# First attention: memory keys turned in 32x32 blocks on VectorE and moved by 16 transfers of ScalarE's queue

## The chip, the cores and the metric

One of the eight cores of one Trainium2 chip runs the kernel. The metric is the device time of one execution in microseconds (us); lower is better. All times of the trace are counted from the start of its span.

## What is computed

The reference is the trunk of a streaming encoder: 256 tokens of width 1024, two layers, each with a half-step FFN, a mixer with `w_in` and `w_out`, and a second half-step FFN. The mixer of the first layer is a pooling mixer. Beside it, in both layers, four heads of 64 attend to 256 rows of a memory. The change touches this attention in the first layer only:

```python
def memory_attention(q, mem, mem_norm_g, w_mem_kv, q_norm_g, k_norm_g):
    B, M, _ = mem.shape
    kv = rms_norm(mem, mem_norm_g) @ w_mem_kv
    k, v = jnp.split(kv.reshape(B, M, 2 * MEM_HEADS, HEAD_DIM), 2, axis=2)
    q = rms_norm(q, q_norm_g)
    k = rms_norm(k, k_norm_g)
    logits = jnp.einsum('bshd,bmhd->bhsm', q, k).astype(jnp.float32) * (HEAD_DIM ** -0.5)
    p = jax.nn.softmax(logits, axis=-1)
    out = jnp.einsum('bhsm,bmhd->bshd', p.astype(v.dtype), v)
    return out.reshape(B, q.shape[1], MEM_WIDTH)
```

Everything is float32. The score product contracts over the 64 values of a head, so queries and keys must both lie with the head's values on the partitions: that is what turning them is for.

## The kernel before

Each engine runs its own list of instructions, written out by hand in the order of the program, and waits on semaphores for the others. TensorE does the matrix products; every large one is done as three products of a high and a low part of either operand. A weight unit is four 128x512 pieces: SyncE loads it (`w_raw`), ScalarE makes the high part (`high_unit`, line 743), VectorE the low part (`low_unit`, line 1156), in three slots used in rotation.

Tokens are in two tiles of 128 (`t` = 0, 1). The stages around the change are, in TensorE's order:

- `mkv0`: the memory's keys and values. VectorE scales them into `mkv_sb` (`kv_copy`, line 1397), sums the squares of the keys (`head_sums`, lines 1406 and 1407), GpSimd makes the roots (`head_roots`), and VectorE scales the keys in place (`head_scale("mk0")`, line 1415).
- `z0b`: the columns of `w_in` that hold the last part of the pooling input and the memory queries. ScalarE copies them out of PSUM in `z_copy(0, 1, t)`: line 956 is the queries, line 957 the pooling part, and line 957 counts up `z_ready`.
- `z0a`: the other columns, tile 0 then tile 1, each eight chunks `k` of three products (lines 1861 to 1863). Two hooks sit in it. `memory_heads(k)`, in tile 0, turns the queries at `k == 3` with `turn_heads(0)` (four 128x128 transposes, line 2056), for which it waits for `mkv_ready` and for `z_ready` at 2, that is for both `z_copy(0, 1, t)`. At `k == 6` it turns the keys with `turn_heads(1)`. `memory_scores(k)`, in tile 1 at `k == 0`, waits for `headT_ready` at 2 and issues the scores (line 2081).
- Between them `head_copy(y)` on ScalarE (line 926) brings the turned queries (`mqT`) and keys (`mkT`) out of PSUM with their gain, each with one count of `headT_ready`.

The table `HEADTS` lists the blocks that `turn_heads` and `head_copy` handle: the name, the PSUM bank and the gain column; `HEADREADY` lists the blocks for which `head_ready` is counted.

The second layer's shared keys already go the other way: VectorE transposes 32x32 blocks into `ycat` (line 1695), GpSimd moves the blocks with 64 transfers within SBUF (line 721), and `key_copy` on ScalarE brings them into `kT` (line 932).

ScalarE's part of the order of work, which is also the order in which its transfers are issued:

```python
high_unit("z0a", 0)
z_copy(0, 1, 0)
high_unit("z0a", 1)
z_copy(0, 1, 1)
high_unit("out0", 0)
head_copy(0)
head_copy(1)
z_copy(0, 0, 0)
```

Of the kernel before, what the change touches and what calls it, by code (L numbers as in the profile page):

```python
# [11 lines left out]
ACT = mybir.ActivationFunctionType  # L12
# [114 lines left out]

HEADNORMS = ["mk0", "mq0", "k1", "mk1", "qa1", "qm1"]
HEADSUMS = ["mk0", "mq0", "k1", ("qa1", 0), ("qa1", 1), "mk1", ("qm1", 0), ("qm1", 1)]
HEADREADY = ["mk0", "k1", "mk1"]  # L130

HEADTS = [("mq0", 7, 1), ("mk0", 6, 0), ("mk1", 1, 3)]

QUERIES = [(0, 0), (0, 1), (1, 0), (1, 1)]
QUERY_BANK = (6, 7, 1, 3)
# [60 lines left out]
def encoder_kernel(nc, a, out):  # L196

    with ExitStack() as ctx:
        def sb(name, shape, dt=F32):
            return ctx.enter_context(nc.sbuf_tensor(name, shape, dt))  # L200

        def sem(name):
            return ctx.enter_context(nc.semaphore(name))
# [11 lines left out]
        mem_blocks = z[:, :, :].rearrange("p t d -> p (t d)").rearrange("p (k t) -> p k t", t=S)  # L215
        key_blocks = ycat[:, 0, 0:NT * KVH * HD].rearrange("p (t c) -> p t c", t=NT)
        key_rows = ycat[:, 1, :].rearrange("p (n t) -> p n t", n=KVH)
        both = sb("mainT", [P, KC, 2, S], F32R)
        tr_hi = {n: sb(f"{n}T_hi", [P, KC, S], F32R) for n in ("side", "y")}
        tr_lo = {n: sb(f"{n}T_lo", [P, KC, S], F32R) for n in ("side", "y")}  # L220
# [63 lines left out]
        mem_blocks_landed = sem("mem_blocks_landed")  # L284
        mem_blocks_turned = sem("mem_blocks_turned")
        keys_landed = sem("keys_landed")
        consts_landed = sem("consts_landed")
        ident_landed = sem("ident_landed")
        gains_landed = [sem(f"gains_landed{g}") for g in range(2)]
# [443 lines left out]
        def _(act):  # L733
# [32 lines left out]
            def high_unit(name, m, halves=(0, 1)):  # L766
                high(name, UNIT[name, m], unit_part(name, m)[1], halves)
# [150 lines left out]
            def head_copy(y):  # L918

                name, bank, g = HEADTS[y]  # L920
                if y == 0:
                    act.wait_ge(consts_landed, 16 * SMALL_LOADS)
                    act.wait_ge(ones_ready, 5)
                act.wait_ge(head_turned, y + 1)
                src, dst = ps[:, bank, :], mqT if name == "mq0" else mkT
                nc.scalar.activation(dst[:, :, :].rearrange("p n t -> p (n t)"), src, ACT.Copy,
                                     scale=head_gain_col[:, g:g + 1]).then_inc(headT_ready, 1)

            def key_copy():

                act.wait_ge(keys_landed, 16 * KVH * BLOCKS * BLOCKS)
                nc.scalar.activation(kT[:, :, :], key_rows, ACT.Copy, scale=head_gain_col[:, 2:3]).then_inc(headT_ready, 1)
# [13 lines left out]
            def z_copy(l, n, t):  # L946
                norm = "H2" if l == 0 else "H7"
                done = Z_ORDER.index((l, n)) + 1
                product_done(act, t, z_done, done, column_units(f"z{l}{'ab'[n]}", n)[1])
                if done % 2 == 1:  # L950
                    act.wait_ge(row_scaled, row_scaled_no(norm, t))
                scale, src, cols = row_scale(norm, t), ps[:, z_bank(l, t, n), :], slice(n * 512, (n + 1) * 512)
                if l == 0 and n == 0:
                    ins = nc.scalar.activation(zp_hi[:, t, cols], src, ACT.Copy, scale=scale)
                elif l == 0:
                    nc.scalar.activation(z[:, t, MIXER:D], src[:, MIXER - 512:512], ACT.Copy, scale=scale)
                    ins = nc.scalar.activation(zp_hi[:, t, 512:MIXER], src[:, 0:MIXER - 512], ACT.Copy, scale=scale)
                else:
                    ins = nc.scalar.activation(z[:, t, cols], src, ACT.Copy, scale=scale)
                ins.then_inc(z_ready, 1)  # L960
# [95 lines left out]
            high_unit("z0a", 0)  # L1056
            z_copy(0, 1, 0)
            high_unit("z0a", 1)
            z_copy(0, 1, 1)
            high_unit("out0", 0)  # L1060
            head_copy(0)
            head_copy(1)
            z_copy(0, 0, 0)
            table_of(ACT.Exp)
            exponentials(0)
# [49 lines left out]
            z_copy(1, 1, 0)  # L1115
            query_squares(1, 0)
            turned_copy(ACT_COPIED)
            head_copy(2)
            high_unit("out1", 1, (0,))
            query_copy(1, 0)  # L1120
            z_copy(1, 1, 1)
# [19 lines left out]
        def _(dve):  # L1141
# [267 lines left out]
            def head_scale(name):  # L1409

                v = head_view(name)
                nh = v.shape[2]
                rs = head_rs[:, HEADNORMS.index(name), 0:NT * nh].rearrange("p (t n) -> p t n", t=NT)
                dve.wait_ge(head_scaled, head_no(name))
                return nc.vector.tensor_tensor(v, v, rs.unsqueeze(3).to_broadcast([P, NT, nh, HD]), ALU.mult)
# [230 lines left out]
            dve.wait_ge(mkv_ready, NT)  # L1646
            head_sums("mk0")
            low_unit("z0a", 0)
            head_scale("mk0").then_inc(head_ready, 1)
            low_unit("z0a", 1)  # L1650
            dve.wait_ge(z_ready, NT)
            head_sums("mq0")
# [96 lines left out]
        def _(pe):  # L1749
# [537 lines left out]
            def memory_heads(k):  # L2287
                if k == 3:
                    pe.wait_ge(mkv_ready, NT)
                    turn_heads(0)  # L2290
                elif k == 6:
                    turn_heads(1)

            def memory_scores(k):
                if k == 0:
# [43 lines left out]
            def second_turns(k):  # L2339
                if k == 0:  # L2340
                    turn_probs(2)
                elif k == 4:
                    turn_probs(3)
                    turn_heads(2)
                elif k == 6:
                    pe.wait_ge(headT_ready, 4)
                    turn_query(1, 0)
# [81 lines left out]
```

## Time and profile before

| | |
|---|---|
| Median of 3 runs | 908.78 us (908.64 to 908.98) |
| Profiled execution: time | 909.13 us |
| Profiled execution: span | 906.9 us |
| TensorE busy | 901.7 us, 99% of the span |
| VectorE busy | 643.2 us, 71% |
| ScalarE busy | 500.8 us, 55% |
| GpSimd busy | 108.8 us, 12% |
| TensorE's share of the chain that ended last | 99% |

The time of an execution is 2.2 us more than its span; the span runs from the first to the last instruction of the trace. A busy share of 99% says that TensorE has matrix products under way nearly always, not that each is at its peak. The chain that ended last is followed back from the last instruction, at each step to what released it.

### The profile page before, as it was taken

To read this page: it belongs to the slowest core of one execution; us is meant where nothing else is said; L and a number is where in the kernel's file an instruction comes from. 1 tells how busy PE (TensorE), PEld (TensorE's weight loads), DVE (VectorE), ACT (ScalarE), POOL (GpSimd) and SP (SyncE) were. 2 spreads that over 40 slices of the span, in tenths; PEclk is the share of its full clock that TensorE was granted. 3 is DMA by queue.
4 is the path that set the end of the run, shared out by engine and by line. 5 is a ranking of instruction groups with operands and counts; after the bars stand their busy time and mean duration, and the time that the engine had idled before them with its cause. 6 is when DMAs were issued, how large, how long until landed. Compare 5 with 4: busy or idle time off the path is not lost.

```text
span 906.9 us, 15027 instructions
## 1 busy us (share of the span) xinstructions
PE 901.7 (99%) x4965; PEld 766.9 (85%) x4965; DVE 643.2 (71%) x1006; ACT 500.8 (55%) x749; POOL 108.8 (12%) x187
## 2 busy tenths in 40 slices
PE   9999999999999999999999999999999999999998
PEld 6888888888888888888888888888888888888887
DVE  6876567687678766566788766666888786666665
ACT  7654545565655554454564645445686664544542
POOL 2153302003000000000002930000132000000000
PEclk9999999999999999999999999999999999999999
DMA  9897666656346656565465865655443276565551
GB/s 303 260 294 219 197 194 177 193 161 203 91 140 206 213 174 196 185 193 194 123 210 165 265 203 166 218 187 182 143 140 118 86 244 215 175 210 189 172 169 47
DMA packets 140180, 168.27 MB, mean 186 GB/s; under 512 B 12472, under 2 KB 104608, under 8 KB 140144
## 3 DMA queue, kind: packets, MB, share of 16 engines
q1 hardware_dynamic: 135600, 164.67, 57.0%
q0 software_dynamic: 4368, 3.07, 1.6%
q8 instruction: 20, 0.33, 0.1%
q14 instruction: 16, 0.13, 0.0%
q10 hardware_dynamic: 176, 0.07, 0.0%
HBM read 166.19 MB, written 1.05 MB: 184 GB/s over the span
## 4 chain that ended last, share of the span: by engine, by line
PE 99%; DVE 1%; ACT 0%; issue 0%; POOL 0%; POOLq 0%
PE ps L1779 35%; PE ps L1784 18%; PE ps L1988 8%; PE ps L1986 8%; PE ps L1984 8%; PE ps L1861 5%; PE ps L1863 5%; PE ps L1862 5%; PE ps L1754 1%; PE ps L2112 1%; PE ps L2216 1%; PE ps L1818 1%; PE ps L2270 0%; PE ps L2081 0%; PE ps L1832 0%; PE ps L2124 0%
## 5 line engine op out<-in xcount | busy, mean ns | idle before, releaser
L1779 PE MATMUL ps<-mainT,w_hi 128*128 128x512 f32 x1376 | 467.7, 392 | 0.1
L1156 DVE TENSOR_TENSOR w_lo<-w_raw,w_hi 128x1024 fp32r<-128x1024 f32 x296 | 350.5, 1221 | 41.3 <-ACT w_hi L743 40.9
L1784 PE MATMUL ps<-mainT,w_lo 128*128 128x256 f32 x1376 | 350.5, 280 | 0.0
L743 ACT CAST w_hi<-w_raw 128x1024 fp32r<-128x1024 f32 x296 | 299.4, 1047 | 29.2 <-PE ps L1779 11.0
L1779 PEld LDWEIGHTS ps<-mainT,w_hi 128*128 128x128 f32 x1376 | 249.2, 187 | 46.1 <-issue 0.5
L1784 PEld LDWEIGHTS ps<-mainT,w_lo 128*128 128x128 f32 x1376 | 255.9, 189 | 13.8
L814 ACT COPY gate_up_f<-ps 128x512 f32<-128x512 f32 x88 | 51.1, 581 | 109.7 <-PE ps L1779 104.0
L1988 PE MATMUL ps<-w_hi,actT_lo 128*128 128x512 f32 x320 | 98.9, 390 | 0.0
L1986 PE MATMUL ps<-w_lo,actT_hi 128*128 128x512 f32 x320 | 98.9, 390 | 0.0
L1984 PE MATMUL ps<-w_hi,actT_hi 128*128 128x512 f32 x320 | 98.6, 389 | 0.0
L1258 DVE TENSOR_TENSOR gate_up_f<-ps,gate_up_f 128x256 f32<-128x256 f32 x88 | 37.3, 423 | 86.1 <-ACT gate_up_f L814 86.0
L820 ACT ACTIVATE gate_up_f<-gate_up_f 128x256 f32<-128x256 f32 x88 | 36.7, 418 | 106.2 <-DVE gate_up_f L1267 106.1
L1281 DVE TENSOR_TENSOR actT_lo<-gate_up_f,actT_hi 128x512 fp32r<-128x512 f32 x40 | 27.7, 692 | 63.9 <-ACT actT_hi L827 63.9
L1988 PEld LDWEIGHTS ps<-w_hi,actT_lo 128*128 128x128 f32 x320 | 60.1, 188 | 12.9
L1986 PEld LDWEIGHTS ps<-w_lo,actT_hi 128*128 128x128 f32 x320 | 60.1, 188 | 12.6
L1984 PEld LDWEIGHTS ps<-w_hi,actT_hi 128*128 128x128 f32 x320 | 60.1, 188 | 11.5
L827 ACT CAST actT_hi<-gate_up_f 128x512 fp32r<-128x512 f32 x40 | 24.8, 620 | 75.1 <-PE ps L1988 69.8
L635 POOL TENSOR_SCALAR row_ms<-row_ss 128x1 f32<-128x1 f32 x14 | 4.9, 349 | 439.8 <-ACT probs L784 439.7
L1275 DVE SCALAR_TENSOR_TENSOR gate_up_f<-gate_up_f 128x256 f32<-128x256 f32 x88 | 37.1, 422 | 22.9 <-ACT gate_up_f L820 22.7
L1267 DVE TENSOR_TENSOR gate_up_f<-gate_up_f,pT 128x256 f32<-128x256 f32 x88 | 36.5, 416 | 0.0
L1260 DVE TENSOR_TENSOR gate_up_f<-ps,gate_up_f 128x256 f32<-128x256 f32 x88 | 36.5, 415 | 0.0
L721 POOL DMA_DIRECT2D ycat<-ycat x64 | 33.9, 538 | 3.0 <-DVE ycat L1695 3.0
(250 smaller groups left out, 845.6 us busy)
## 6 DMA issues: line engine op xcount, KB each, us to landing
w_raw<-in_ffn_w_gate_up_dram SPq DMA_DIRECT2D x352, 256.0 KB, 3.9
w_raw<-in_ffn_w_down_dram SPq DMA_DIRECT2D x176, 256.0 KB, 3.4
w_raw<-in_w_in_dram SPq DMA_DIRECT2D x32, 256.0 KB, 3.4
w_raw<-in_w_out_dram SPq DMA_DIRECT2D x32, 256.0 KB, 3.3
w_raw<-in_w_mem_kv_dram SPq DMA_DIRECT2D x16, 256.0 KB, 3.2
w_raw<-in_w_kv_dram SPq DMA_DIRECT2D x8, 256.0 KB, 3.6
ycat<-in_mem_dram SPq DMA_DIRECT2D x1, 1024.0 KB, 9.0
z<-in_mem_dram POOLq DMA_DIRECT2D x32, 32.0 KB, 4.0
```

The source lines that it names most:

```text
L743: ins = nc.scalar.copy(half(w_hi[s], b), half(w_raw[s], b))
L814: nc.scalar.copy(gate_up_f[:, :, fb, :], ps[:, GU_BANK + 2 * fb:GU_BANK + 2 * fb + 2, S:2 * S]).then_inc(parts_copied, 1)
L1156: ins = nc.vector.tensor_tensor(half(w_lo[s], b), half(w_raw[s], b), half(w_hi[s], b).bitcast(F32), ALU.subtract)
L1258: nc.vector.tensor_tensor(silu_g[:, fb, :], ps[:, bank, 0:S], silu_g[:, fb, :], ALU.add).then_inc(gate_summed, 1)
L1779: return pe.matmul(gate_sums(fb, j)[:, :, tokens], w_hi[units[k // 4][0]][:, k % 4, cols], both[:, k, :, tokens], start=start, stop=stop)
L1784: return pe.matmul(gate_sums(fb, j)[:, 0, tokens], w_lo[units[k // 4][0]][:, k % 4, cols], both[:, k, 0, tokens], start=False, stop=False)
L1861: pe.matmul(dst, x_hi, wh, start=start, stop=False)
L1862: pe.matmul(dst, x_hi, wl, start=False, stop=False)
L1863: return pe.matmul(dst, x_lo, wh, start=False, stop=stop)
L1984: pe.matmul(dst[n], xh, wh[n], start=first and fc == 0, stop=False)
L1986: pe.matmul(dst[n], xh, wl[n], start=False, stop=False)
L1988: mm = pe.matmul(dst[n], xl, wh[n], start=False, stop=closes and (t, n) == (1, 1))
```

## The change

After `head_scale` VectorE transposes the keys of the first attention in 32x32 blocks, all 128x512 of them in one instruction, into the first half of `ycat`. ScalarE then issues 16 transfers of one block row and column each (32 partitions, 4 runs of 32 values, 128 bytes a run) that put the blocks in their place in the second half of `ycat`, and copies them with the gain into `mkT`. The four transposes of the keys on TensorE and the `head_copy` of them go. The transfers are issued between `high_unit("z0a", 1)` and `z_copy(0, 1, 1)`. Where `HEADTS` and `HEADREADY` lose an entry, the numbers of the later entries move up by one; the counts of `headT_ready` stay as they were.

```diff
@@ -127,9 +127,9 @@
 
 HEADNORMS = ["mk0", "mq0", "k1", "mk1", "qa1", "qm1"]
 HEADSUMS = ["mk0", "mq0", "k1", ("qa1", 0), ("qa1", 1), "mk1", ("qm1", 0), ("qm1", 1)]
-HEADREADY = ["mk0", "k1", "mk1"]
-
-HEADTS = [("mq0", 7, 1), ("mk0", 6, 0), ("mk1", 1, 3)]
+HEADREADY = ["k1", "mk1"]
+
+HEADTS = [("mq0", 7, 1), ("mk1", 1, 3)]
 
 QUERIES = [(0, 0), (0, 1), (1, 0), (1, 1)]
 QUERY_BANK = (6, 7, 1, 3)
@@ -215,6 +215,8 @@
         mem_blocks = z[:, :, :].rearrange("p t d -> p (t d)").rearrange("p (k t) -> p k t", t=S)
         key_blocks = ycat[:, 0, 0:NT * KVH * HD].rearrange("p (t c) -> p t c", t=NT)
         key_rows = ycat[:, 1, :].rearrange("p (n t) -> p n t", n=KVH)
+        memory_blocks = ycat[:, 0, 0:NT * MEMH * HD].rearrange("p (n c) -> p n c", c=P)
+        memory_rows = ycat[:, 1, 0:NT * MEMH * HD].rearrange("p (n c) -> p n c", c=P)
         both = sb("mainT", [P, KC, 2, S], F32R)
         tr_hi = {n: sb(f"{n}T_hi", [P, KC, S], F32R) for n in ("side", "y")}
         tr_lo = {n: sb(f"{n}T_lo", [P, KC, S], F32R) for n in ("side", "y")}
@@ -284,6 +286,8 @@
         mem_blocks_landed = sem("mem_blocks_landed")
         mem_blocks_turned = sem("mem_blocks_turned")
         keys_landed = sem("keys_landed")
+        memory_keys_turned = sem("memory_keys_turned")
+        memory_keys_landed = sem("memory_keys_landed")
         consts_landed = sem("consts_landed")
         ident_landed = sem("ident_landed")
         gains_landed = [sem(f"gains_landed{g}") for g in range(2)]
@@ -926,6 +930,22 @@
                 nc.scalar.activation(dst[:, :, :].rearrange("p n t -> p (n t)"), src, ACT.Copy,
                                      scale=head_gain_col[:, g:g + 1]).then_inc(headT_ready, 1)
 
+            def memory_keys():
+
+                act.wait_ge(memory_keys_turned, 1)
+                for i in range(BLOCKS):
+                    for j in range(BLOCKS):
+                        nc.scalar.dma_start(memory_rows[j * BLOCK:(j + 1) * BLOCK, :, i * BLOCK:(i + 1) * BLOCK],
+                                            memory_blocks[i * BLOCK:(i + 1) * BLOCK, :, j * BLOCK:(j + 1) * BLOCK]).then_inc(
+                            memory_keys_landed, 16)
+
+            def memory_key_copy():
+
+                act.wait_ge(memory_keys_landed, 16 * BLOCKS * BLOCKS)
+                nc.scalar.activation(mkT[:, :, :].rearrange("p n (t c) -> p t n c", t=NT),
+                                     memory_rows.rearrange("p (t n) c -> p t n c", t=NT), ACT.Copy,
+                                     scale=head_gain_col[:, 0:1]).then_inc(headT_ready, 1)
+
             def key_copy():
 
                 act.wait_ge(keys_landed, 16 * KVH * BLOCKS * BLOCKS)
@@ -1056,10 +1076,11 @@
             high_unit("z0a", 0)
             z_copy(0, 1, 0)
             high_unit("z0a", 1)
+            memory_keys()
             z_copy(0, 1, 1)
             high_unit("out0", 0)
             head_copy(0)
-            head_copy(1)
+            memory_key_copy()
             z_copy(0, 0, 0)
             table_of(ACT.Exp)
             exponentials(0)
@@ -1115,7 +1136,7 @@
             z_copy(1, 1, 0)
             query_squares(1, 0)
             turned_copy(ACT_COPIED)
-            head_copy(2)
+            head_copy(1)
             high_unit("out1", 1, (0,))
             query_copy(1, 0)
             z_copy(1, 1, 1)
@@ -1646,7 +1667,9 @@
             dve.wait_ge(mkv_ready, NT)
             head_sums("mk0")
             low_unit("z0a", 0)
-            head_scale("mk0").then_inc(head_ready, 1)
+            link(head_scale("mk0"))
+            nc.vector.transpose(memory_blocks.rearrange("p (t n) c -> p t (n c)", t=NT),
+                                mkv_sb[:, :, 0:MEMH * HD]).then_inc(memory_keys_turned, 1)
             low_unit("z0a", 1)
             dve.wait_ge(z_ready, NT)
             head_sums("mq0")
@@ -2288,8 +2311,6 @@
                 if k == 3:
                     pe.wait_ge(mkv_ready, NT)
                     turn_heads(0)
-                elif k == 6:
-                    turn_heads(1)
 
             def memory_scores(k):
                 if k == 0:
@@ -2341,7 +2362,7 @@
                     turn_probs(2)
                 elif k == 4:
                     turn_probs(3)
-                    turn_heads(2)
+                    turn_heads(1)
                 elif k == 6:
                     pe.wait_ge(headT_ready, 4)
                     turn_query(1, 0)
```

ScalarE's list at the place of the change, before. Line 956 with line 957 is `z_copy(0, 1, 1)`, line 743 `high_unit`, line 926 `head_copy`:

```order
L743 CAST w_hi<-w_raw 128x1024 [waits weights_used0,raw_landed00]
L743 CAST w_hi<-w_raw 128x1024 [waits weights_used0,raw_landed01]
L956 ACTIVATE z<-ps,row_rs 128x256 [waits row_scaled,weights_used1]
L957 ACTIVATE yT_hi<-ps,row_rs 128x256
L743 CAST w_hi<-w_raw 128x1024 [waits weights_used1,raw_landed10]
L743 CAST w_hi<-w_raw 128x1024 [waits weights_used1,raw_landed11]
L926 ACTIVATE mqT<-ps,head_gain_col 128x512 [waits head_turned,ones_ready,consts_landed]
L926 ACTIVATE mkT<-ps,head_gain_col 128x512 [waits head_turned]
L954 ACTIVATE yT_hi<-ps,row_rs 128x512 [waits z_done]
```

The same place in the change. Its lines 976 and 977 are `z_copy(0, 1, 1)`, line 747 `high_unit`, line 938 `memory_keys`, line 930 `head_copy(0)`, line 945 `memory_key_copy`:

```order
L747 CAST w_hi<-w_raw 128x1024 [waits weights_used0,raw_landed00]
L747 CAST w_hi<-w_raw 128x1024 [waits weights_used0,raw_landed01]
L938 DMA ycat<-ycat 32x4x32 [waits memory_keys_turned]
L938 DMA ycat<-ycat 32x4x32 x15
L976 ACTIVATE z<-ps,row_rs 128x256 [waits row_scaled,weights_used1]
L977 ACTIVATE yT_hi<-ps,row_rs 128x256
L747 CAST w_hi<-w_raw 128x1024 [waits weights_used1,raw_landed10]
L747 CAST w_hi<-w_raw 128x1024 [waits weights_used1,raw_landed11]
L930 ACTIVATE mqT<-ps,head_gain_col 128x512 [waits head_turned,ones_ready,consts_landed]
L945 ACTIVATE mkT<-ycat,head_gain_col 128x2x2x128 [waits memory_keys_landed]
L974 ACTIVATE yT_hi<-ps,row_rs 128x512 [waits z_done]
```

The sixteen transfers stand ahead of `z_copy(0, 1, 1)`, which counts up `z_ready`; the copy of the keys waits for their landing and no longer for TensorE.

TensorE's list in `z0a`, tile 0, around the hooks of chunk 3 and chunk 6, before. Line 2056 is `turn_heads`, here of the keys; lines 1861 to 1863 are the products:

```order
L1863 MATMUL ps<-w_hi,mainT 128x512
L2056 MATMUL ps<-ident,mkv_sb 128x128 [waits head_ready]
L2056 MATMUL ps<-ident,mkv_sb 128x128 x3
L1861 MATMUL ps<-w_hi,mainT 128x512 [waits lo_ready0]
L1862 MATMUL ps<-w_lo,mainT 128x512
L1863 MATMUL ps<-w_hi,mainT 128x512
```

The same stretch in the change, where line 2079 is `turn_heads` and lines 1884 to 1886 are the products, and behind it the hook of chunk 3, three chunks earlier:

```order
L1884 MATMUL ps<-w_hi,mainT 128x512
L1885 MATMUL ps<-w_lo,mainT 128x512
L1886 MATMUL ps<-w_hi,mainT 128x512
L1884 MATMUL ps<-w_hi,mainT 128x512 [waits lo_ready0]
L1885 MATMUL ps<-w_lo,mainT 128x512
L1886 MATMUL ps<-w_hi,mainT 128x512
```

```order
L1886 MATMUL ps<-w_hi,mainT 128x512
L2079 MATMUL ps<-ident,z 128x128 [waits z_ready,mkv_ready]
L2079 MATMUL ps<-ident,z 128x128 x3
L1884 MATMUL ps<-w_hi,mainT 128x512
L1885 MATMUL ps<-w_lo,mainT 128x512
L1886 MATMUL ps<-w_hi,mainT 128x512
```

The four transposes of the keys and their wait for `head_ready` are gone. The four transposes of the queries, with their wait for `z_ready`, stand where they stood before.

VectorE's list in the change, where line 1436 is `head_scale("mk0")`, line 1671 the new transpose of 32x32 blocks and line 1177 `low_unit`:

```order
L1177 TENSOR_TENSOR w_lo<-w_raw,w_hi 128x1024 [waits hi_ready2] x2
L1436 TENSOR_TENSOR mkv_sb<-mkv_sb,head_rs 128x2x256 [waits head_scaled]
L1671 STREAM_TRANSPOSE ycat<-mkv_sb 128x512 [waits dve_step]
L1177 TENSOR_TENSOR w_lo<-w_raw,w_hi 128x1024 [waits hi_ready0] x2
L1427 TENSOR_TENSOR gate_up_f<-z 128x512 [waits z_ready]
```

Before, `low_unit("z0a", 1)` followed on `head_scale` directly; one instruction, with a wait for VectorE's own `head_scale`, is added between them.

## Rows read from the trace of the kernel before

**Rows 1.** Chain of waits that ended last, share of the span by engine.

```profile
PE 99%; DVE 1%; ACT 0%; issue 0%; POOL 0%; POOLq 0%
```

**Rows 2.** Timeline, ScalarE: start us, us, engine line op, tiles, count [idle before <-releaser].

```profile
212.91 1.05 ACT L743 CAST w_hi<-w_raw 128x1024 fp32r<-128x1024 f32 x1 [0.31 <-PE ps L1863]
215.58 0.47 ACT L956 ACTIVATE z<-ps,row_rs 128x256 f32<-128x256 f32 x1 [1.61 <-PE ps L1863]
215.95 0.47 ACT L957 ACTIVATE yT_hi<-ps,row_rs 128x256 fp32r<-128x256 f32 x1
216.31 1.99 ACT L743 CAST w_hi<-w_raw 128x1024 fp32r<-128x1024 f32 x2
218.19 0.70 ACT L926 ACTIVATE mqT<-ps,head_gain_col 128x512 f32<-128x512 f32 x1
220.58 0.69 ACT L926 ACTIVATE mkT<-ps,head_gain_col 128x512 f32<-128x512 f32 x1 [1.69 <-PE ps L2056]
```

**Rows 3.** Timeline, TensorE, z0a tile 0 to the scores, and the start of out0.

```profile
217.19 0.39 PE L1863 MATMUL ps<-w_hi,mainT 128*128 128x512 f32 x1
217.42 0.60 PE L2056 MATMUL ps<-ident,z 128*128 128x128 f32 x4
...
219.94 0.60 PE L2056 MATMUL ps<-ident,mkv_sb 128*128 128x128 f32 x4
220.30 0.48 PE L1861 MATMUL ps<-w_hi,mainT 128*128 128x512 f32 x1
220.62 0.39 PE L1862 MATMUL ps<-w_lo,mainT 128*128 128x512 f32 x1
220.85 0.40 PE L1863 MATMUL ps<-w_hi,mainT 128*128 128x512 f32 x1
...
221.87 2.00 PE L2081 MATMUL ps<-mkT,mqT 64*128 64x256 f32 x16
...
241.06 0.50 PE L1861 MATMUL ps<-w_hi,yT_hi 128*128 128x512 f32 x1
```

**Rows 4.** Timeline, VectorE, keys to the first maximum of the scores.

```profile
210.80 1.08 DVE L1415 TENSOR_TENSOR mkv_sb<-mkv_sb,head_rs 128x512 f32<-128x512 f32 x1 [1.54 <-POOL head_rs L647]
212.63 2.59 DVE L1156 TENSOR_TENSOR w_lo<-w_raw,w_hi 128x1024 fp32r<-128x1024 f32 x2 [0.76 <-ACT w_hi L743]
216.45 0.69 DVE L1406 TENSOR_TENSOR gate_up_f<-z 128x512 f32<-128x512 f32 x1 [1.23 <-ACT yT_hi L957]
...
223.08 1.23 DVE L1496 TENSOR_REDUCE row_max<-ps 128x4 f32<-128x1024 f32 x1 [2.17 <-PE ps L2081]
```

**Rows 5.** One line's instructions, line 1695: count, ns min/median/max, when.

```profile
L1695 DVE STREAM_TRANSPOSE ycat<-kv_sb x1: 711/711/711, 494.9 to 494.9; 128x512 f32<-128x512 f32 x1
```

**Rows 6.** The same view, lines 1004 and 1005: transfers issued on ScalarE's queue.

```profile
L1004 ACTq DMA_DIRECT2D ident<-in_c_ident_dram x1: 403/403/403, 0.7 to 0.7; - x1
DMA to landing us min/median/max: 2.7/2.7/2.7
L1005 ACTq DMA_DIRECT2D pT<-in_ffn_norm_dram x1: 447/447/447, 1.2 to 1.2; - x1
```

**Rows 7.** Timeline, SyncE and ScalarE: back-to-back issues, and what follows them.

```profile
1.65 1.28 ACT L1007 ACT_TABLE_LOAD   x1 [1.65 <-PEq L2419]
8.95 4.79 SPq L540 DMA_DIRECT2D w_raw<-in_ffn_w_gate_up_dram  x8
```

**Rows 8.** One line's instructions, line 540: transfers on SyncE's queue.

```profile
L540 SPq DMA_DIRECT2D w_raw<-in_w_out_dram x32: 327/380/440, 203.8 to 684.0; - x32
```

**Rows 9.** One line's instructions, line 721: the 64 transfers within SBUF.

```profile
L721 POOL DMA_DIRECT2D ycat<-ycat x64: 536/536/647, 495.9 to 529.2; - x64
DMA to landing us min/median/max: 1.6/3.1/4.4
```

**Rows 10.** Transfers by line and size: tiles, queue, count, KB each, us to landing.

```profile
ident<-in_c_ident_dram ACTq DMA_DIRECT2D x1, 64.0 KB, 2.7
pT<-in_ffn_norm_dram ACTq DMA_DIRECT2D x1, 8.0 KB, 2.6
```

**Rows 11.** Chain of waits that ended last, start of the kernel: start us, us, what.

```profile
1.32 2.74 PE ps L2270 x6
5.32 1.34 PE ps L2270 x4
```

**Rows 12.** Windows: stretch, us, busy (x) of PE, PEld, DVE, ACT, POOL, PEclk, DMA, GB/s.

```profile
2.00:3.00 1.00, 1.00 (x4) 0.30 (x2) 0.00 (x0) 0.99 (x2) 0.73 (x2) 1.00 0.70 231
217.40:221.90 4.50, 4.50 (x26) 3.49 (x24) 3.51 (x5) 2.18 (x3) 1.84 (x2) 1.00 0.47 154
```

**Rows 13.** Waits from 8 to 16 us: who for whom, us, times, longest.

```profile
PE ps L1818 <- DVE mainT L1194: 0.8, 1, 0.8
```

## The prediction

> **What bounds the kernel now.** I read the page first: TensorE carries 99% of the chain that ended last [rows 1]. So whatever takes TensorE's time, or makes it stand still, is paid in full, and work of the other engines costs only where TensorE ends up waiting for it. Next I read the timelines of the three engines between 210 and 224 us. TensorE [rows 3] runs through without a gap: products, the four transposes of the queries at 217.42, more products, the four transposes of the keys at 219.94, and the scores at 221.87. ScalarE [rows 2] is what it has to be watched against. It is often idle there, but its idle time lies in places: it is free at 213.96 (212.91 + 1.05) and next works at 215.58, on `z_copy(0, 1, 1)`, whose second part ends at 216.42 (215.95 + 0.47). TensorE asks for that result at 217.42. The margin between them is 1.0 us, and this number decides the case. VectorE [rows 4] scales the keys until 211.88 and is then idle until 212.63.
>
> **What the change removes.** The four transposes of the keys go from TensorE's own list. They and the slower start behind them take from 219.94 to the third product at 220.85 minus two products of 0.227 us (the pitch of the rows without transposes, for instance 217.19 to 217.42): 0.91 - 0.46 = 0.45 us. All of it is on the path: **-0.45 us**. The `head_copy` of the keys on ScalarE (0.69 us) goes too, and a copy of the same size from SBUF takes its place; I take 0.7 us for it. No gain or loss there, since ScalarE waited 1.69 us ahead of it [rows 2].
>
> **What it adds on VectorE.** One transpose of 128x512 in 32x32 blocks. The same instruction on the other keys took 0.711 us [rows 5]. It runs from 211.9, when `head_scale` has ended, to about 212.65. The next instruction started at 212.63, after 0.76 us of idle time, so it slips by less than 0.1 us, and its result, which ended at 215.22, is wanted by TensorE only for chunk 4, behind the transposes of 217.42 [rows 3, 4]. Cost nothing. If that cover were gone, the price would be the 0.75 us.
>
> **What it adds on ScalarE.** The blocks are turned at about 212.65, before ScalarE arrives at 213.96, so it finds its semaphore up and begins to issue at once. Sixteen issues stand between 213.96 and `z_copy(0, 1, 1)`. What does one cost? The two transfers that ScalarE issued itself took 0.403 and 0.447 us, the second began at 1.2 us and the next instruction of the engine started at 1.65, right behind it [rows 6, 7]: ScalarE is held for the whole of an issue and does nothing else meanwhile. On SyncE single issues took 0.327 to 0.440 us, and eight back to back 4.79 us, 0.60 each, at a time when large loads filled the DMA engines [rows 7, 8]. GpSimd's 64 transfers of the same kind took 0.536 each [rows 9], but GpSimd is another engine. These are the bounds: 0.33 and 0.60 us. I take 0.44 with the gap to the next, as the rows of the same queue are nearest. Sixteen of them are 7.0 us, so `z_copy(0, 1, 1)` starts at 221.0 instead of 215.58. It takes 0.84 us (215.58 to 216.42), and TensorE sees `z_ready` at about 221.9.
>
> The Trainium skill (DMA: Bandwidth & Descriptors, Issuing engines are not separate DMA queues) says otherwise: the sequencer's time to start a DMA "is usually small relative to the DMA itself". Taken as a reason to count the issues at nothing, it would make the whole sum -0.45 us, and 908.3 us in all.
>
> **The stall.** TensorE stands at the hook of chunk 3 from 217.42 to 221.9: **+4.5 us**. Everything behind it on TensorE waits too: the rest of `z0a`, the scores, the pooling. From there the chain of the first attention is 217.42 to 221.87 less the removed 0.45, so 4.0 us, and the scores can start at 225.9.
>
> **Is something else late then?** Four things move with ScalarE, and each is compared with 225.9 or what follows it.
> - The copies. `high_unit("out0", 0)` 221.85 to 223.7 and the copy of the queries to 224.4 come first [rows 2]. The last transfer is issued at 220.6. ScalarE's own transfer landed 2.7 us after its issue [rows 6], those within SBUF after 1.6 to 4.4 us, median 3.1 [rows 9]: 223.3 to 225.0. The copy of the keys then ends at 225.1 to 225.7. Hidden, with 0.2 to 0.8 us to spare.
> - VectorE. Its `head_sums("mq0")` waited for the same `z_copy` and moves by 5.4 us; the first maximum had 2.17 us of idle time before it [rows 4], and moves by 4.05 with TensorE. 2.17 - (5.4 - 4.05) leaves 0.8 us. Hidden.
> - GpSimd's roots of the queries are needed at the end of that maximum, later still. Hidden.
> - SyncE's loads of `out0` move with the low parts on VectorE by 5.4 us; those units are used from 241 us on [rows 3]. Hidden.
>
> **Sum.** 4.5 - 0.45 = +4.05 us. Against the profiled execution, 909.13 + 4.05 = 913.2; that execution is 0.35 us above the median of the runs, so the median after is 908.78 + 4.05 = **912.8 us**, 0.45% slower. With the bounds of one issue: 16 x 0.33 gives +2.3 us (911.1), 16 x 0.60 gives +6.6 (915.4). About 0.2%, or 1.8 us, is what a measurement of this kernel can tell from no change.
>
> **Rivals.**
>
> *An issue is cheap for ScalarE (not slower).* If the queue took transfers without holding the engine, `z_copy` would not be late. The point is 0.156 us an issue: (216.5 - 213.96)/16. Below it the change gains its 0.45 us, 908.3. Up to 0.30 us an issue the loss is within 1.8 us. For it: the transfers are small, 16 KB each, where the loads are 256 KB. Against it: ScalarE's transfers of 64 and 8 KB took 0.403 and 0.447 us, so size hardly matters [rows 6, 10]. Chance 8%. The rule of the Trainium skill's page DMA: Bandwidth & Descriptors that is quoted above would lead to this case; two rows of this very queue speak against it.
>
> *The clock of TensorE falls in the stall.* No row shows a standstill of such length: the longest behind the first microseconds is 0.8 us [rows 13], and the granted clock is 1.00, the 2.4 GHz level, throughout [rows 12]. But at the very start, when TensorE comes from rest, six products of 128x512 took 2.74 us, 0.46 each, against 0.227 later, and the four that followed 1.34 us [rows 11], though the granted clock reads 1.00 there too [rows 12]. Products at half pace cost 2.74 - 6 x 0.227 = 1.4 us and 1.34 - 0.91 = 0.4 us, about 2 us with the transposes between. If the stall does the same, the time is 912.8 + 2 = 914.8 us. The Trainium skill (TensorE: Matmul & The Clock Gate, Why this matters for your kernels) warns of idle gaps between bursts for this reason, and by it this case is the one to expect once the gap is long enough; no row here says whether 4.5 us are. Chance 27%.
>
> *The landing is late.* Sixteen transfers of 128 runs of 128 bytes share the DMA engines with SyncE's loads. If the last lands over 4.5 us after its issue, the scores wait for `mkT`; each microsecond later costs one. With 6 us it would be +5.5, 914.3. The 64 transfers of the other keys landed within 4.4 us beside SyncE's loads [rows 9]. Chance 8%.
>
> *A partial fall of the cost*, between 0.16 and 0.30 us an issue, is in the first rival's 8%. The forecast itself, with issues of 0.33 to 0.60 us and nothing else late, has 57%.
>
> **Numbers.** Range 911.1 to 916.0: the low end is the cheapest issue that a row shows, the high end the clock's fall behind issues of about 0.5 us. Below it lies most of the first rival, above it a fall of the clock with the dearest issues. Slower by over 0.2%: 57 + 27 + 8 = 92%, less 1 for ends of these cases near the bound: 91%. Within 0.2%: 8%. Faster: 1%, since the whole gain in sight is 0.45 us.
>
> **What would show it.** In the profile after: 16 issues on ScalarE's queue from about 214 to 221 us; `z_copy(0, 1, 1)` at 221.0; TensorE idle for about 4.5 us ahead of the transposes of `z`, released by ScalarE's copy; scores right behind `z0a`'s tile 0 with no gap of their own; VectorE's `head_sums("mq0")` idle for over 5 us before. The forecast is wrong in its main step if the issues take under 0.3 us each, or if `z_copy` starts before they are done. The granted clock behind the stall, and the pitch of the products (0.227 or about 0.46 us), decide on the clock. A wait of line 2104 for the copy of the keys would decide for the late landing.

## The result, and the profile after

The changed kernel takes 918.11 us (median of 4 runs, 917.21 to 918.45) against 908.88 us before (4 runs, 908.64 to 909.46). The ratio is 1.0098 with a 95% interval of 1.0086 to 1.011: 9.2 us slower. The prediction was 912.8 us with a range to 916.0. It had the sign and the place, and less than half of the size.

| | before | after |
|---|---|---|
| Profiled execution: time | 909.13 us | 918.41 us |
| Profiled execution: span | 906.9 us | 916.2 us |
| TensorE's share of the chain that ended last | 99% | 97%, and 1% ScalarE's queue |
| Issues on ScalarE's queue in the first attention | none | 16, together 10.95 us |
| Mean granted clock of TensorE | 1.000 | 0.994 |

Timeline of ScalarE after (columns as in [rows 2], to which these rows answer; `ACTq` is its queue of transfers):

```profile
212.66 1.06 ACT L747 CAST w_hi<-w_raw 128x1024 fp32r<-128x1024 f32 x1 [0.30 <-PE ps L1886]
212.68 10.95 ACTq L938 DMA_DIRECT2D ycat<-ycat  x16
223.74 0.47 ACT L976 ACTIVATE z<-ps,row_rs 128x256 f32<-128x256 f32 x1 [10.02 <-issue]
...
226.93 0.73 ACT L945 ACTIVATE mkT<-ycat,head_gain_col 128x512 f32<-128x512 f32 x1
```

The instructions of line 938 (count, ns min/median/max, when):

```profile
L938 ACTq DMA_DIRECT2D ycat<-ycat x16: 608/623/754, 212.7 to 223.0; - x16
...
DMA to landing us min/median/max: 1.8/2.2/3.7
```

One issue took 0.62 us, and from one to the next it is 10.95/16 = 0.684 us. From the end of the cast (212.66 + 1.06 = 213.72) on ScalarE computed nothing until the issues were through: `z_copy(0, 1, 1)` began at 223.74, where it had begun at 215.58 [rows 2]. The issues began at 212.68, while the cast that stands ahead of them in the list was still running. So the first issue does not wait for the arithmetic ahead of it, but what stands behind the issues waits for all of them.

Timeline of TensorE after (it answers to [rows 3]):

```profile
216.94 0.39 PE L1886 MATMUL ps<-w_hi,mainT 128*128 128x512 f32 x1
224.72 1.08 PE L2079 MATMUL ps<-ident,z 128*128 128x128 f32 x4 [7.40 <-ACT yT_hi L977]
...
226.03 0.63 PE L1885 MATMUL ps<-w_lo,mainT 128*128 128x512 f32 x1
226.46 0.63 PE L1886 MATMUL ps<-w_hi,mainT 128*128 128x512 f32 x1
...
230.44 0.39 PE L1884 MATMUL ps<-w_hi,mainT 128*128 128x512 f32 x1
230.67 0.40 PE L1885 MATMUL ps<-w_lo,mainT 128*128 128x512 f32 x1
...
231.23 2.00 PE L2104 MATMUL ps<-mkT,mqT 64*128 64x256 f32 x16
```

And its windows of one microsecond (columns as in [rows 12]; the granted clock stands behind POOL's count):

```profile
219.00:220.00 1.00, 0.00 (x0) 0.00 (x0) 0.00 (x0) 0.00 (x0) 0.00 (x0) 0.92 0.38 84
220.00:221.00 1.00, 0.00 (x0) 0.00 (x0) 0.00 (x0) 0.00 (x0) 0.00 (x0) 0.50 0.20 30
...
229.00:230.00 1.00, 1.00 (x4) 0.79 (x3) 0.08 (x1) 0.00 (x0) 0.00 (x0) 0.50 0.85 295
230.00:231.00 1.00, 1.00 (x6) 0.73 (x4) 0.00 (x0) 0.00 (x0) 0.00 (x0) 0.96 0.77 277
```

TensorE was due for the transposes of the queries at 217.17 (216.94 + 0.227), stood still until 224.72, and then worked at a pitch of 0.43 us a product until about 230, and at 0.23 again from there. The granted clock went from 1.00 (2.4 GHz) to 0.50 (1.2 GHz) just before 220, with TensorE idle, and came back at about 230, after some 5 us of products.

This gives the account of the stretch from the transposes to the scores. Before it lasted 221.87 - 217.42 = 4.45 us [rows 3]. After, counted from when it was due, 231.23 - 217.17 = 14.06 us. The difference of 9.61 us is a standstill of 224.72 - 217.17 = 7.55, less 0.45 for the transposes that went, and what is left is 2.51 us of slow transposes and products. The profiled execution came to this stretch 0.25 us earlier than the one before, and 9.61 - 0.25 = 9.4 agrees with the difference of the spans, 9.3. Nothing worth naming is gained or lost behind the scores.

### The profile page after: what moved, and what is told of

It reads as the page before. It is cut to its first block, busy times and chain, and to the rows that moved or that the text cites. A ratio compares the mean times of both kernels' runs of the same rounds, so it can differ in the third digit from the quotient of the medians.

```text
span 916.2 us, 15036 instructions
## 1 busy us (share of the span) xinstructions
PE 903.5 (99%) x4961; PEld 768.1 (84%) x4961; DVE 643.7 (70%) x1007; ACT 501.1 (55%) x749; POOL 108.8 (12%) x187
## 4 chain that ended last, share of the span: by engine, by line
PE 97%; ACTq 1%; DVE 1%; ACT 0%; issue 0%; POOL 0%; POOLq 0%
PE ps L1802 34%; PE ps L1807 18%; PE ps L2011 8%; PE ps L2009 8%; PE ps L2007 8%; PE ps L1884 5%; PE ps L1886 5%; PE ps L1885 5%; PE ps L1777 1%; ACTq L938 1%; PE ps L2135 1%; PE ps L1841 1%; PE ps L2239 1%; PE ps L2104 0%; PE ps L1855 0%; PE ps L2293 0%
```

## The experiments

All are edits of the changed kernel, so line numbers of theirs are near its own. The ratios are to the kernel before. The theory under test, A, is the account above: ScalarE is held for 0.68 us by each issue, TensorE stands still for a result behind them, and the clock falls in the standstill.

### TensorE kept at work in the standstill

```diff
                 if k == 3:
                     pe.wait_ge(mkv_ready, NT)
+                    keep_warm(32)
                     turn_heads(0)
```

> The change with 32 dummy products (128x512, zeros, into a free PSUM bank) on TensorE right ahead of the turning of the queries, where it stands still. They take 32 x 0.227 = 7.3 us and fit in the standstill of 7.4 us. Theory A (the products behind the standstill ran at half pace only because the clock fell while TensorE was idle): the granted clock stays 1.00, the products behind keep the 0.227 us pitch, and the time falls by 2.5 us against the change, to 915.6 us. Theory B (the slow pace comes from what the other engines do when they all start again): the clock or the pitch is as slow as before behind the dummies, and the time stays at 918.1 us.

Measured: 915.91 us (ratio 1.0075, 1.0059 to 1.0092), 2.2 us less than the change. TensorE's timeline and one of its windows:

```profile
217.48 6.85 PE L2293 MATMUL ps<-probs 128*128 128x512 bf16 x31
224.57 0.66 PE L2079 MATMUL ps<-ident,z 128*128 128x128 f32 x4 [0.24 <-ACT yT_hi L977]
...
228.60 2.00 PE L2104 MATMUL ps<-mkT,mqT 64*128 64x256 f32 x16
```

```profile
224.00:226.00 2.00, 1.75 (x10) 1.25 (x9) 1.41 (x3) 2.00 (x4) 0.00 (x0) 1.00 0.05 8
```

The first line is the dummy products. The transposes begin at nearly the same time as in the change, since ScalarE is as late, but the clock stays at 1.00 and the scores follow 4.03 us behind (228.60 - 224.57) and not 6.51. So 2.5 us of the loss in the profiled execution are the clock's (2.2 us between the medians), and theory B, that the other engines slow TensorE down, is out.

### Fewer transfers

```diff
                 for i in range(BLOCKS):
-                    for j in range(BLOCKS):
+                    for j in (i ^ 1, i ^ 2):
...
-                act.wait_ge(memory_keys_landed, 16 * BLOCKS * BLOCKS)
+                act.wait_ge(memory_keys_landed, 16 * 8)
```

> The change with 8 of the 16 transfers (the blocks on the diagonal and those three off it are left out, so half of the keys do not reach their place). Theory A (every issue holds ScalarE for 0.68 us and that alone makes the standstill): z_copy starts 5.5 us after the first issue instead of 11.1, TensorE stands still for about 2.1 us instead of 7.4, the clock stays at 1.00 in so short a standstill, and the time is 908.9 + 2.1 - 0.45 = 910.5 us. Theory C (a fixed cost of the first transfers, or of the wait for the turned blocks, makes most of it): the standstill falls by clearly less than 5.5 us and the time stays above 912.

With twelve, `j` runs over `(i ^ 1, i ^ 2, i ^ 3)`:

> The change with 12 of the 16 transfers (the blocks on the diagonal are left out, a quarter of the keys). Theory A: a standstill of 7.5 - 4 x 0.68 = 4.8 us, about the one the prediction had. If the clock falls in it, as it fell about 2.6 us after the last product in the change, the time is 908.9 + 4.8 - 0.45 + 2.5 = 915.7 us or a little less; if a standstill of that length leaves the clock alone, 913.2 us. Theory C: above 916.

Measured: eight transfers 910.53 us (ratio 1.0016, 1.0006 to 1.0025), twelve 915.98 us (1.0073, 1.0056 to 1.009). Timelines of ScalarE and TensorE with eight, then with twelve:

```profile
213.21 5.30 ACTq L938 DMA_DIRECT2D ycat<-ycat  x8
...
217.47 0.39 PE L1886 MATMUL ps<-w_hi,mainT 128*128 128x512 f32 x1
219.60 0.63 PE L2079 MATMUL ps<-ident,z 128*128 128x128 f32 x4 [1.75 <-ACT yT_hi L977]
...
223.60 2.00 PE L2104 MATMUL ps<-mkT,mqT 64*128 64x256 f32 x16
```

```profile
213.76 8.21 ACTq L938 DMA_DIRECT2D ycat<-ycat  x12
...
218.01 0.39 PE L1886 MATMUL ps<-w_hi,mainT 128*128 128x512 f32 x1
223.06 1.09 PE L2079 MATMUL ps<-ident,z 128*128 128x128 f32 x4 [4.66 <-ACT yT_hi L977]
...
228.99 2.00 PE L2104 MATMUL ps<-mkT,mqT 64*128 64x256 f32 x16
```

Eight issues take 5.30 us and twelve 8.21: 0.66 and 0.68 each, so the cost is per issue, with no fixed part that shows, and theory C is out. The standstills, by the starts, are 1.9 us and 4.8 us. The clock, a window in the short one and then two in the long one:

```profile
219.00:220.00 1.00, 0.40 (x5) 0.43 (x5) 0.51 (x1) 1.00 (x3) 0.00 (x0) 1.00 0.85 239
```

```profile
220.00:221.00 1.00, 0.00 (x0) 0.00 (x0) 0.00 (x0) 0.00 (x0) 0.00 (x0) 0.68 0.71 165
221.00:222.00 1.00, 0.00 (x0) 0.00 (x0) 0.00 (x0) 0.00 (x0) 0.00 (x0) 0.50 0.21 33
```

Over the short standstill it stayed at 1.00, and the time is what theory A gave, 910.5. In the long one, which has about the length that the prediction had reckoned with, it fell. From the transposes to the scores it took 223.60 - 219.60 = 4.00 us with eight and 228.99 - 223.06 = 5.93 with twelve, so the fall cost 1.9 us here. The 915.7 expected for twelve reckoned with 2.5; that 915.98 came out near it is in part luck, for the profiled execution had also come to the stretch 0.8 us later than the one before.

### What one issue costs

```diff
-                for i in range(BLOCKS):
-                    for j in range(BLOCKS):
-                        nc.scalar.dma_start(memory_rows[j * BLOCK:(j + 1) * BLOCK, :, i * BLOCK:(i + 1) * BLOCK],
...
+                for k in range(3):
+                    nc.scalar.dma_start(memory_rows[k * BLOCK:(k + 1) * BLOCK, :, 0:BLOCK],
+                                        memory_blocks[0:BLOCK, :, k * BLOCK:(k + 1) * BLOCK]).then_inc(memory_keys_landed, 16)
...
+                for k in range(3):
+                    nc.scalar.dma_start(ycat[32:64, 1, 512 + k * P:512 + (k + 1) * P],
+                                        a["mem"][0][0:BLOCK, k * P:(k + 1) * P]).then_inc(memory_keys_landed, 16)
```

> The change with 21 transfers in seven forms, three each, in place of the 16 (the keys do not reach their place; what is measured is what an issue of each form takes on ScalarE's queue). Theory D (the price comes from several runs a partition on both sides): about 0.62 us with 4 runs of 128 bytes a partition on both sides, less with one side in one run, about 0.4 with one run on either side, whether 32 or 128 partitions, SBUF or DRAM. Theory E (it comes from SBUF as the source): 0.62 for all that stay within SBUF, 0.4 for the two that read DRAM. Theory F (it comes from the number of descriptors, 128 a transfer): 0.62 for the forms with 128 runs, and clearly less for 32 runs of 512 bytes; against it stands the transfer of the identity, 128 runs at 0.403 us.

The instructions by line, in the order of issue. Lines 937 to 949 stay within SBUF: the change's own form; 4 runs a partition into one; 32 partitions with one run of 512 bytes; 128 partitions with 128 bytes; 128 partitions with 512 bytes. Lines 952 and 955 read DRAM, with one run and with 4 runs a partition:

```profile
L937 ACTq DMA_DIRECT2D ycat<-ycat x3: 616/635/772, 213.1 to 214.6; - x3
L940 ACTq DMA_DIRECT2D ycat<-ycat x3: 622/623/624, 215.2 to 216.5; - x3
L943 ACTq DMA_DIRECT2D ycat<-ycat x3: 612/612/620, 217.2 to 218.5; - x3
L946 ACTq DMA_DIRECT2D ycat<-ycat x3: 472/616/627, 219.1 to 220.7; - x3
L949 ACTq DMA_DIRECT2D ycat<-ycat x3: 622/622/623, 221.2 to 222.5; - x3
L952 ACTq DMA_DIRECT2D ycat<-in_mem_dram x3: 437/443/603, 223.2 to 224.3; - x3
L955 ACTq DMA_DIRECT2D ycat<-in_mem_dram x3: 445/453/453, 224.8 to 225.7; - x3
```

Neither the runs nor the partitions nor the bytes matter by the medians; theories D and F are out. What is left is whether DRAM is on one side, or else the time of the issue, since those from DRAM stood last. A single execution took 920.83 us, with 21 issues ahead of `z_copy`.

The same with the order turned round, and a store to DRAM added:

> Transfers in five forms, three each, on ScalarE's queue in place of the 16, now with those that read DRAM first, while SyncE loads weights, and the change's own form last (the keys do not reach their place). The first such run gave 0.62 us for every form from SBUF to SBUF and 0.44 for the two from DRAM, but those stood last. Theory E2 (SBUF on both sides costs 0.62): DRAM to SBUF 0.44 here too, SBUF to DRAM 0.33 to 0.44 as SyncE's five stores of the result take, SBUF to SBUF 0.62. Theory I (the price falls with time or when SyncE's loads end): the first forms take 0.62 and the change's own form, standing last, 0.44.

The instructions by line, in the order of issue: 937 from DRAM with 4 runs a partition, 940 from DRAM with one run, 943 a store into the output in DRAM (32 partitions, one run of 512 bytes), 946 within SBUF with one run, 949 the change's own form:

```profile
L937 ACTq DMA_DIRECT2D ycat<-in_mem_dram x3: 339/456/521, 212.9 to 213.8; - x3
L940 ACTq DMA_DIRECT2D ycat<-in_mem_dram x3: 443/443/451, 214.3 to 215.3; - x3
L943 ACTq DMA_DIRECT2D out_dram<-ycat x3: 442/443/444, 215.7 to 216.7; - x3
L946 ACTq DMA_DIRECT2D ycat<-ycat x3: 519/610/635, 217.2 to 218.8; - x3
L949 ACTq DMA_DIRECT2D ycat<-ycat x3: 622/622/679, 219.3 to 220.7; - x3
```

The order does not matter, and theory I is out: medians of 0.44 to 0.46 us with DRAM on either side, 0.61 to 0.62 with SBUF on both. SBUF as the source alone does not do it, as the store shows. There are three transfers of each form in one execution, so these are prices of this place in the kernel; what makes an issue from SBUF to SBUF dearer stays open. A single execution took 915.87 us. This is why the two rows that the prediction took its price from [rows 6] misled it: they are transfers from DRAM.

### The transfers behind the copy

```diff
-            memory_keys()
             z_copy(0, 1, 1)
-            high_unit("out0", 0)
+            memory_keys()
             head_copy(0)
+            high_unit("out0", 0)
             memory_key_copy()
```

> The change with its 16 transfers issued behind z_copy(0, 1, 1) and not ahead of it, the copy of the queries next and high_unit(out0, 0) last before the copy of the keys. Theory A (what costs is that ScalarE is held for 16 x 0.68 = 10.9 us, wherever the issues stand, since TensorE wants the keys from ScalarE 5 us behind the queries): the turning of the queries is on time, and TensorE stands still at the scores, from about 221.4 us, for 9 us until about 230.5, with the clock falling in it: 908.9 + 9.1 - 0.45 + 2.4 = 920 us. Theory G (only the place in ScalarE's list was wrong): behind z_copy the transfers are hidden, and the time is 908.5 us.

Measured: 918.99 us (ratio 1.0109, 1.0095 to 1.0124). The standstill is only moved; from the timelines of ScalarE and TensorE:

```profile
215.31 0.73 ACTq L938 DMA_DIRECT2D ycat<-ycat  x1
...
217.15 0.60 PE L2079 MATMUL ps<-ident,z 128*128 128x128 f32 x4
...
229.51 3.78 PE L2104 MATMUL ps<-mkT,mqT 64*128 64x256 f32 x16 [8.31 <-ACT mkT L945]
```

Theory G is out. The time is 1 us below what theory A gave, and so are the scores, at 229.5 and not at 230.5: the first issue began at 215.31, with `z_copy` still running.

### All transfers on GpSimd's queue

The 16 transfers stand in GpSimd's list behind its copies of the band tables and ahead of `head_roots("mq0")`; `memory_keys` issues nothing on ScalarE.

> The change with all 16 transfers on GpSimd's queue, behind its band copies and ahead of the roots of the memory queries; ScalarE issues none. Theory A: z_copy is on time and TensorE turns the queries without waiting. GpSimd issues from 212.9 for 16 x 0.56 = 9.0 us, the last lands about 2 us behind its issue, at 223.3, and the keys are in mkT at 224.1, where TensorE asks for them at 221.4: a standstill of 2.7 us at the scores, 908.9 + 2.7 - 0.45 = 911.2 us. Whether the clock falls in 2.7 us lies between what two runs showed (no fall at 1.75 us, a fall at 4.66): if it does, up to 2.4 us more, 913.5. If the queue mattered and not the number of issues ahead of a wanted result, the time would be 908.5.

Measured: 914.24 us (ratio 1.0055, 1.0038 to 1.0072). From the timelines of GpSimd, ScalarE and TensorE:

```profile
212.52 8.76 POOL L531 DMA_DIRECT2D ycat<-ycat  x16
...
224.76 0.72 ACT L956 ACTIVATE mkT<-ycat,head_gain_col 128x512 f32<-128x512 f32 x1 [6.23 <-DMA ycat<-ycat]
...
225.53 3.78 PE L2115 MATMUL ps<-mkT,mqT 64*128 64x256 f32 x16 [4.47 <-ACT mkT L956]
```

```profile
224.00:225.00 1.00, 0.00 (x0) 0.00 (x0) 0.00 (x0) 0.24 (x1) 0.00 (x0) 0.50 0.40 154
```

The turning of the queries was on time, as theory A has it, and the issues took what was expected. The landing took longer: the last transfer was issued at 220.7 and ScalarE could copy at 224.8, 4.0 us later and not 2. So the standstill was 4.47 us, and the clock fell in it (0.69 in the microsecond from 223, 0.50 from 224 to 230). Even off ScalarE, sixteen issues in one queue, 8.76 us, and a landing of up to 4.0 us are too long for a result that TensorE wanted at about 220.9, 8.4 us after the first issue.

### The transfers dealt out to three queues

```diff
-                for i in range(BLOCKS):
-                    for j in range(BLOCKS):
...
+                move_keys(nc.scalar, MOVES[0:4])
...
+                    if name == "out0":
+                        sp.wait_ge(memory_keys_turned, 1)
+                        move_keys(sp, MOVES[4:10], moved["sp"])
                     for m in range(2, n):
                         load_dense(name, m)
...
             nc.gpsimd.tensor_copy(band1_r, band1).then_inc(band_ready, 1)
+            pool.wait_ge(memory_keys_turned, 1)
+            move_keys(pool, MOVES[10:16], moved["pool"])
```

> The change with the 16 transfers dealt out: 4 on ScalarE's queue at the same place, 6 on SyncE's ahead of the last two units of out0, 6 on GpSimd's behind its band copies. Theory A: 4 issues of 0.68 us run from about 212.7 to 215.4, beside the cast that ends at 214 and in the idle time ahead of z_copy, which is on time; the others issue until about 216.5 and land before 220; TensorE never stands still, the four transposes stay saved, and the time is 908.9 - 0.45 = 908.5 us, 0.05% faster. Theory H (what costs is the transfers themselves, their landing or their load on the DMA engines): the scores still wait and the time stays above 911.

Measured: 908.05 us (11 runs, 907.70 to 908.64) against 909.16 us (23 runs); ratio 0.999, interval 0.9981 to 0.9999. The issues by queue, and ScalarE and TensorE:

```profile
L531 SPq DMA_DIRECT2D ycat<-ycat x6: 601/604/717, 212.3 to 215.6; - x6
L531 POOL DMA_DIRECT2D ycat<-ycat x6: 548/548/651, 212.6 to 215.4; - x6
L531 ACTq DMA_DIRECT2D ycat<-ycat x4: 616/625/732, 212.6 to 214.7; - x4
```

```profile
215.39 0.47 ACT L990 ACTIVATE z<-ps,row_rs 128x256 f32<-128x256 f32 x1 [1.76 <-PE ps L1900]
...
217.08 0.60 PE L2093 MATMUL ps<-ident,z 128*128 128x128 f32 x4
...
221.06 2.00 PE L2118 MATMUL ps<-mkT,mqT 64*128 64x256 f32 x16
```

`z_copy(0, 1, 1)` waits for TensorE again and not for the issues, TensorE has no standstill, and from the transposes to the scores it takes 3.98 us, 0.47 less than before [rows 3]. The same 16 transfers cost nothing here, so theory H is out. This version is faster than the change by about 10 us and faster than the kernel before by very little: the interval ends just below 1. Of the 1.1 us between the medians the trace explains the 0.47. Another 0.4 us lie outside the span: the time was 1.8 to 1.9 us more than the span in every execution here and with all transfers on GpSimd's queue, and 2.2 to 2.3 us before. No run shows why.

### No transfers, VectorE alone

```diff
-            nc.vector.transpose(memory_blocks.rearrange("p (t n) c -> p t (n c)", t=NT),
-                                mkv_sb[:, :, 0:MEMH * HD]).then_inc(memory_keys_turned, 1)
+            for i in range(BLOCKS):
+                for j in range(BLOCKS):
+                    ins = nc.vector.transpose(
+                        memory_rows.rearrange("p (t n) c -> p t n c", t=NT)[quadrant(j), :, :, quadrant(i)],
+                        mkv_sb[:, :, 0:MEMH * HD].rearrange("p t (n c) -> p t n c", c=P)[quadrant(i), :, :, quadrant(j)])
+            ins.then_inc(memory_keys_turned, 1)
```

> The change without any transfer: VectorE writes the 16 blocks of 32 partitions straight into their place, in 16 transposes of 32 partitions by 128 values in place of the one of 128x512. One of them should take about 0.23 us (those of 32x64 in this kernel take 0.232), so 3.5 to 4 us in VectorE's list at 211.7. Theory A: ScalarE is free, z_copy is on time, the low parts of z0a's second unit come at about 217.9 just in time for chunk 4 at 218, and the time is 908.9 - 0.45 = 908.5 us. Rival: the low parts come late by a microsecond or VectorE is late for the first maximum, and the time is 909 to 910.

Measured: 909.49 us (12 runs, one of which took 3167.84 us and does not enter the ratio; ratio 1.0005, 0.9996 to 1.0014), no difference that can be told. From one transpose of 32x128 to the next it was 0.316 us (5.05/16), not 0.23, and VectorE reached the first maximum at 223.85, 2.2 us behind the start of the scores and not 1.2 as before [rows 3, 4]. The line of TensorE between them is the start of the scores:

```profile
212.12 5.05 DVE L1672 STREAM_TRANSPOSE ycat<-mkv_sb 32x128 f32<-32x128 f32 x16
...
221.63 2.00 PE L2107 MATMUL ps<-mkT,mqT 64*128 64x256 f32 x16
...
223.85 1.22 DVE L1516 TENSOR_REDUCE row_max<-ps 128x4 f32<-128x1024 f32 x1
```

The rival came true: VectorE is late for the first maximum, and behind it TensorE waits 0.6 us for the weights of the attention (`probs`), a wait that the trace of before does not have. This eats the 0.45 us.

## Why the prediction was wrong in size

The step that failed is the price of one issue: the sum had 0.44 us and 0.684 were measured. A second term, the fall of the clock, stood in the sum at nothing and took 2.5 us. Against the 4.05 us of the sum the longer standstill makes 7.55 - 4.5 = 3.05 more and the clock 2.51, together the 9.61 us of the stretch.

- **What bounds the kernel, and the place.** Right. The margin of 1 us between `z_copy(0, 1, 1)` and TensorE decides, the issues stand ahead of it, and what they take beyond ScalarE's idle time and that margin is paid: 10.95 us of issues made 7.55 us of standstill.
- **The removed transposes, -0.45 us.** Right: 3.98 us against 4.45 where nothing else disturbs (three queues).
- **VectorE's transpose hidden.** Right. It ran from 211.65 for 0.71 us, and the low parts behind it were on time.
- **The price of an issue: this step failed.** The sum took 0.44 us from the two rows of ScalarE's own queue as the nearest, and set 0.33 and 0.60 as bounds. Measured: 0.62 an issue, 0.684 from one to the next, above the upper bound. "The rows of the same queue are nearest" was the wrong reading: they load from DRAM, and the two runs with forms show that a transfer with SBUF on both sides costs 0.17 us more on this queue whatever its shape. The rows of GpSimd's 64 transfers [rows 9] were nearer in kind; they would have given 0.54, still too little. The upper bound, 0.60, came from loads from DRAM on SyncE's queue [rows 7], so DRAM on one side does not make an issue cheap on every queue. The issues also began at 212.68, beside the cast and not behind it at 213.96, which gave a microsecond back. The standstill was 7.55 us and not 4.5.
- **The clock.** Told as a rival with 27%, it happened. By the runs with twelve transfers and with all of them on GpSimd's queue it also falls in standstills of 4.66 and 4.47 us, about the 4.5 us that the sum itself forecast, so the term belonged into the sum even with issues of 0.44 us. It cost 2.5 us. The rival's 2 us came near that with some luck: they were read from products at half pace at the start of the kernel [rows 11], where the granted clock read 1.00 [rows 12], while here the half pace went with a granted clock of 0.50. The rule of the Trainium skill (TensorE: Matmul & The Clock Gate, Why this matters for your kernels), that idle gaps between bursts bring the clock down, agrees with this case's trace: the granted clock was 0.50 from 220 to 230 us.
- **A combination without a price.** The range ended at 916.0. The prediction put "a fall of the clock with the dearest issues" above it, but gave it neither a time nor a chance; by its own terms it was 915.4 + 2 = 917.4, near the 918.1 measured. Without the fall the measured price gives 915.9, as the run with TensorE kept at work shows. Dearer issues make a longer standstill, and the clock stayed up over 1.75 us and fell in every standstill of 4.47 us or more. The two were weighed as if they were apart.
- **Landing, VectorE, GpSimd, SyncE hidden.** Right: the last transfers had landed when ScalarE came to the copy of the keys at 226.93, right behind the copy of the queries, and there was no wait at the scores. The landing was late only with all transfers on GpSimd's queue, 4.0 us behind the last issue.
- **Cheap issues, 8%.** Did not happen. One issue is short beside the 2.2 us in which a transfer lands, but sixteen of them held ScalarE for 10.95 us.

## What to carry to other kernels

A transfer costs the engine that issues it time of its own, on ScalarE's queue 0.62 us with SBUF on both sides, and 0.68 from one to the next, for 16 KB as for 64 KB: count the issues that stand ahead of a result that somebody wants, and find for each queue the idle stretch they fit into. The standstills of TensorE of 4.47 us and more were dearer than their length, so for such a one the clock's price belongs into the sum, not beside it. Take the price of an instruction from rows with the same source and destination, and not only from the same queue.

## What the runs showed of the hardware

- An issue on ScalarE's queue took 0.44 to 0.46 us (medians) with DRAM on one side and 0.61 to 0.62 us from SBUF to SBUF, with 32 or 128 partitions, 32 or 128 runs, 16 to 64 KB. SyncE's queue took 0.604 us and GpSimd 0.548 us for the same SBUF to SBUF transfer.
- The first of several issues on ScalarE's queue does not wait for the end of the arithmetic ahead of it in the list (212.68, beside a cast from 212.66 to 213.72; 215.31, where the two parts of `z_copy` ahead of it ran from 215.30 to 216.15).
- The granted clock of TensorE stayed at 1.00 over idle times of 1.75 us and fell to 0.50 in those of 4.47, 4.66, 7.40 and 8.31 us. It came back after 4.1 to 5.4 us of work. A fall cost 2.5 us behind the standstill of 7.40 us (2.2 between the medians) and 1.9 us behind that of 4.66.
- Sixteen transposes of 32x128 on VectorE that each write a block of 32 partitions, most of them another than they read, took 5.05 us, 0.316 from one to the next; one of 128x512 within the partitions' own quarter 0.71 us.
